# Retention: the high parts of the query and key weight slabs written by a rounding DMA from GpSimd instead of a ScalarE cast

## The reference

```
def _retention(xn, w_in, subln, w_out):
    B, T, _ = xn.shape
    H, Dk, Dv, C = RT_HEADS, RT_KEY_DIM, RT_VAL_DIM, RT_CHUNK
    proj = xn @ w_in
    q, k, v, g = jnp.split(proj, [H * Dk, 2 * H * Dk, 2 * H * Dk + H * Dv], axis=-1)
    ...
        att = jnp.einsum('bhqd,bhkd->bhqk', qq, kk) * decay_intra
        o = (jnp.einsum('bhqk,bhkv->bhqv', att, vv)
             + jnp.einsum('bhqd,bhdv->bhqv', qq, R) * xi[:, :, None])
    ...
    o = _rms(o, subln).reshape(B, T, H * Dv)
    return (jax.nn.silu(g.astype(jnp.float32)) * o).astype(xn.dtype) @ w_out
```

## Time and profile before

| what | value |
|---|---|
| time, median of 3 runs | 1614.63 us (1613.79 to 1614.81) |
| span of the profiled execution | 1611.9 us |
| TensorE busy | 1603.9 us, 100% |
| VectorE busy | 1050.6 us, 65% |
| ScalarE busy | 854.2 us, 53% |
| GpSimd busy | 45.3 us, 3% |

### The profile page before, as it was taken

The page is one execution under the profiler, slowest core; times in us unless marked ns, Lnnn a source line. Parts: engine busy times, 40 slices in busy tenths (PEclk is TensorE's granted clock), DMA queues, the critical chain, the costliest instruction groups (busy, mean ns, idle before and its releaser), DMA issues.

```text
span 1611.9 us, 22737 instructions
## 1 busy us (share of the span) xinstructions
PE 1603.9 (100%) x8789; PEld 1361.9 (84%) x8789; DVE 1050.6 (65%) x1214; ACT 854.2 (53%) x1079; POOL 45.3 (3%) x50
## 2 busy tenths in 40 slices
PE   9999999999999999999999999999999999999999
PEld 7878888978888888888888888888888888888887
DVE  6766656877656776667777666666667554566665
ACT  6654444785444554446775444554445454554443
POOL 2000000000000030000000000000000000000000
PEclk9999999999999999999999999999999999999999
DMA  9635455424555465454345554455545444445540
GB/s 356 226 118 215 178 207 186 164 104 177 191 207 186 153 222 206 184 184 182 121 181 191 201 193 176 177 209 190 194 177 208 160 179 168 172 153 193 203 182 27
DMA packets 42856, 294.29 MB, mean 183 GB/s; under 512 B 4784, under 2 KB 5344, under 8 KB 8736
## 3 DMA queue, kind: packets, MB, share of 16 engines
q1 hardware_dynamic: 39312, 281.04, 47.3%
q0 software_dynamic: 3184, 12.02, 2.3%
q10 hardware_dynamic: 288, 0.20, 0.0%
HBM read 289.18 MB, written 3.15 MB: 181 GB/s over the span
## 4 chain that ended last, share of the span: by engine, by line
PE 98%; DVE 1%; ACT 1%; issue 0%; POOL 0%; DVEq 0%; ACTq 0%; POOLq 0%
PE ups L293 26%; PE accs L260 15%; PE accs L261 15%; PE accs L262 15%; PE ups L296 13%; PE accs L293 2%; PE ups L498 1%; PE accs L296 1%; PE ups L1420 1%; PE accs L449 1%; PE accs L446 1%; PE accs L451 1%; PE ups L2393 1%; DVE wlo L245 1%; PE ups L1046 1%; PE ups L1057 1%
## 5 line engine op out<-in xcount | busy, mean ns | idle before, releaser
L245 DVE TENSOR_TENSOR wlo<-raw,whi 128x2048 fp32r<-128x2048 f32 x263 | 601.5, 2291 | 205.0 <-ACT whi L241 204.9
L293 PE MATMUL ups<-xhl,whi 128*128 128x512 f32 x1824 | 573.2, 396 | 0.0
L241 ACT CAST whi<-raw 128x2048 fp32r<-128x2048 f32 x265 | 505.5, 1910 | 105.7 <-PE accs L262 105.1
L296 PEld LDWEIGHTS ups<-xhl,wlo 128*128 128x128 f32 x1824 | 342.9, 188 | 79.7
L296 PE MATMUL ups<-xhl,wlo 128*128 128x256 f32 x1824 | 358.4, 278 | 0.0
L293 PEld LDWEIGHTS ups<-xhl,whi 128*128 128x128 f32 x1824 | 282.4, 189 | 5.0
L260 PE MATMUL accs<-whi,hidh 128*128 128x512 f32 x692 | 272.4, 394 | 0.0
L261 PE MATMUL accs<-wlo,hidh 128*128 128x512 f32 x692 | 269.9, 390 | 0.0
L262 PE MATMUL accs<-whi,hidl 128*128 128x512 f32 x692 | 269.6, 390 | 0.0
L262 PEld LDWEIGHTS accs<-whi,hidl 128*128 128x128 f32 x692 | 130.0, 188 | 27.6
L260 PEld LDWEIGHTS accs<-whi,hidh 128*128 128x128 f32 x692 | 129.9, 188 | 24.8 <-issue 1.3
(11 more groups left out here) (275 smaller groups left out, 1406.1 us busy)
## 6 DMA issues: line engine op xcount, KB each, us to landing
raw<-weights SPq DMA_DIRECT2D x265, 1024.0 KB, 4.8
gain<-gains POOLq DMA_DIRECT2D x9, 512.0 KB, 4.0
rel_scratch<-sub_rstd POOLq DMA_DIRECT2D x1, 2048.0 KB, 10.9
big<-rel_scratch POOLq DMA_DIRECT2D x1, 1536.0 KB, 10.4
h<-x_in SPq DMA_DIRECT2D x2, 512.0 KB, 5.1
raw<-weights SPq DMA_DIRECT2D x2, 512.0 KB, 6.3
tabs<-consts POOLq DMA_DIRECT2D x1, 1024.0 KB, 6.6
big<-big POOLq DMA_DIRECT2D x2, 384.0 KB, 4.8
```

Source lines behind the costliest of these rows:

```text
L241: nc.scalar.copy(whi[:, m % SPLIT, :], raw[:, m % RAW, :]).then_inc(hi_ready, 1)
L245: nc.vector.tensor_tensor(wlo[:, m % SPLIT, :], raw[:, m % RAW, :], whi[:, m % SPLIT, :].bitcast(F32), ALU.subtract).then_inc(lo_ready, 1)
L293: mm = nc.tensor.matmul(bank, W(whi, n, k, j * P, (j + 1) * P), xhl[:, k, :, :].rearrange("p a n -> p (a n)"), start=k == 0, stop=False)
L296: mm = nc.tensor.matmul(bank[:, 0:T], W(wlo, n, k, j * P, (j + 1) * P), xh[:, k, :], start=False, stop=k == KC - 1)
```

## The change

For the 8 query and key slabs (`ROUNDED`) ScalarE's cast is left out. GpSimd issues a second load of the same slab from HBM, whose destination is `whi`; the DMA converts float32 to float32r on its way. It waits on `slab_used` for the same value that the cast waited for. ScalarE, in the place where the cast stood, waits until that load has landed, and then counts `hi_ready` up by hand. The plain load into `raw` stays, since VectorE needs it for the low part.

```
+        def load_high(pool, m, turn):
+            pool.wait_ge(slab_used, m - SPLIT + 1)
+            pool.dma_start(whi[:, m % SPLIT, :], weights[m]).then_inc(S(f"high_loaded{turn % 2}"), 16)
+
+        def take_high_load(act, m, turn):
+            act.wait_ge(S(f"high_loaded{turn % 2}"), 16 * (turn // 2 + 1))
+            act.wait_ge(raw_loaded[m % RAW], 16 * (m // RAW + 1))
+            act.wait_ge(hi_ready, m)
+            act.sem_inc(hi_ready, 1)
...
+        ROUNDED = [m for m in range(RT_HEADS * RT_SLABS) if m % RT_SLABS in (2, 3)]
...
             for m in range(RT_HEADS * RT_SLABS):
                 u, j = m // RT_SLABS, m % RT_SLABS
-                split_high(act, n_r + m + 2)
+                if m + 2 in ROUNDED:
+                    take_high_load(act, n_r + m + 2, ROUNDED.index(m + 2))
+                else:
+                    split_high(act, n_r + m + 2)
                 if j == 0 and u >= 1:
                     gates(u - 1)
                 if j == 1 and u >= 1:
                     stats(u - 1)
...
+            for turn, m in enumerate(ROUNDED):
+                load_high(pool, n_r + m, turn)
```

## The result

The changed kernel takes 1622.78 us (median of 4 runs, 1620.24 to 1624.42) beside 1614.72 us: ratio 1.0049, 95% interval 1.0033 to 1.0065, so 8 us slower. In a second series on another occasion it took 1623.94 us (5 runs), ratio 1.0055 [1.0041 to 1.0068]. The forecast was 1621.0 within 1616.8 to 1631.

What follows compares the result with a forecast made beforehand. TensorE, busy without a gap, was taken to bound the kernel; its waits in four heads add 6.4 us to the span, 1611.9 to 1618.3, and 2.7 us up to the median gives 1621.0 us, range 1616.8 to 1631.

Steps and rivals of the forecast that it cites:

- The bound: Retention projections: TensorE busy for all 149 us, so removing eight casts, 15.3 us of ScalarE, is worth nothing by itself.
- The shortest distance: Behind the k wait: gated product to `turn_pair`, 1.4 us in head 1, 1.5 in head 2; value copy to slab 21, 2.9.
- The formulas: TensorE's waits: X - 3.1 in head 1, X - 3.2 in head 2, X - 4.6 in head 3.
- X: GpSimd load's time from issue to landing: 5.2 us plus 0.5 for conversion and partial collisions, 5.7; 6.6 in head 0.
- Where X came from: Bounds from plain loads, 5.2 to 7.8 us; k loads were taken to meet no SP load, so near 5.2.
- Head 0: q load behind the last gain load, low part wanted at 1239.24: a wait of X - 6.4, 0.2 us.
- The clock: None of TensorE's waits was thought long enough for the granted clock to fall.
- The 6.4 us: Sum of TensorE's waits: 2.6 (head 1), 2.5 (head 2), 1.1 (head 3) and 0.2 (head 0).
- the 2.7 us between span and median: The 2.7 us by which the median lies above the profiled span, added to 1618.3 to give 1621.0.
- (1): GpSimd's load lands as fast as SP's, X below 4.7, so the time stays the same; chance 0.14.
- (2): Conversion slows GpSimd's load, X from 7 on; at 7.8 the waits are 13.9 us, 1628.5 us; chance 0.22.
- (3): Distances misread, so the wait is absorbed, or relief of ScalarE speeds matmuls; chance 0.06, of which 0.02 faster.

Runs made afterwards that it cites:

- e1: The changed kernel with only the four q slabs loaded by GpSimd, the k slabs cast by ScalarE: 1615.18 us, ratio 1.0003 to the kernel before.
- e9: e7 with head 0's k slab cast by ScalarE, so seven slabs keep GpSimd's load: 1614.6 us, ratio 0.9999 to the kernel before.
- e3: The changed kernel with statistics (ScalarE) and gated product (VectorE) moved ahead of the k wait and subtraction: 1615.47 us, ratio 1.0004 to the kernel before.
- e5: e4 with ScalarE waiting, after its k cast in heads 1 to 3, for the plain load to land: 1630.76 us, ratio 1.01 to the kernel before.
- e8: e3 without its VectorE edit, so only ScalarE's statistics move ahead of the wait: 1618.35 us, ratio 1.0025 to the kernel before.
- e2: The changed kernel with only the four k slabs loaded by GpSimd, q cast by ScalarE: 1630.64 us, ratio 1.0094 to the kernel before.
- e4: The kernel before, casts kept, plus eight plain GpSimd loads of the q and k slabs into an unread region: 1614.63 us, ratio 0.9997.
- e7: e3 with the last gain load moved behind the first q load on GpSimd: 1620.22 us, ratio 1.0035 to the kernel before.

## Why the prediction was right, point by point

**The bound.** TensorE busy without a pause and ScalarE with time to spare: right. In e1 and e9 ScalarE is busy for 7.8 and 12.3 us less between 1228 and 1377, and nothing is gained.

**The shortest distance.** The wait acts through the work behind it, first the statistics and then the gated product, and lands at `turn_pair`. This is shown by e3 (order changed, loads kept), e5 (wait alone) and e8 (each queue holds back its own part). The formulas, with the X of the first profile: 5.0 - 3.1 = 1.9, 5.5 - 3.2 = 2.3 and 5.0 - 4.6 = 0.4 against 2.1, 2.4 and 0.6. They are 0.1 to 0.2 us short at each place, which would fit a handover on the way that I did not count; no run shows which. In e2 they are 3.8, 5.0 and 2.7 against 3.9, 5.1 and 2.9.

**X.** 5.0 to 5.5 us for the k loads of heads 1 to 3, where 5.7 was taken: the allowance for conversion was not needed. This made the forecast 0.7, 0.2 and 0.7 us too high in the three heads, or 0.5, 0.1 and 0.5 with the handover that it left out. (Where the forecast says of the earlier trace rows that the "first second" shows no traffic, it is the first microsecond.)

**Where X came from.** "The k loads fall where no SP load is in transit" is a misreading, and here the forecast had luck. In the kernel before SP's slab of 1269.88 is under way when the k slot of head 1 is released at 1270.92, and the windows from 1272 to 1274 show 426 GB/s. In the changed kernel the k load was alone only because the q load holds back VectorE's subtraction, and SP with it: its slab is issued at 1276.96 there, 3.2 us behind the k load. The forecast had counted that lateness as costing nothing and gaining nothing. In e2, with the q load gone, the same reading fails: X is 6.9 to 8.2.

**Head 0.** The q load took 7.3 us, where 6.6 was taken, behind the gain load and with SP's beside it. By X - 6.4 that is 0.9; the matmuls waited 0.8 and the weight loads 1.2. Its k load took 8.0, and the weight loads waited 0.3 at slab 3. The forecast had 0.2 for the head.

**The clock.** "None is long enough for me to expect the clock to fall" was the wrong sentence. In one of two profiled executions of the changed kernel it fell, behind both longer gaps, and that execution's span is 2.6 us longer; by the mean granted clock (0.998 or less) it probably did in at least six of nine.

**The number.** The 6.4 us are near the measured 8 to 9 in part because errors cancel. X was too long, by 1.6 us over the three heads. Too short were the handovers (0.5 us), head 0 (0.6 by the matmuls, 1.0 to 1.3 by the weight loads) and the clock, which had nothing and takes some 2.6 us where it falls behind both gaps. And the 2.7 us between span and median are not all "what lies around" the span: executions with a span of 1611.9 took 1613.9, so 2.0 lie around it and 0.7 come from a profiled execution that was quicker than the median one. In the changed kernel 1.8 lie around it (1620.3 and 1622.07).

**The rivals.** (1) Not slower needed X below 4.7: it was never below 5.0, though SP's loads took 4.8. The Trainium skill's fit ("DMA: Bandwidth & Descriptors", Anatomy of one DMA) of 4.4 us for 1 MiB from GpSimd is below every one of these loads; these traces decide for 5.0. (2) Slow conversion: not so, by e4. Wherever X was 6.4 us or more, SP's queue moved 0.57 MB or more during the load. That alone does not stretch it, though: in e4 the k load of head 1 landed in 5.0 us with 0.92 MB of SP's in the same stretch, most of it ahead of GpSimd's data. (3) The distances were those read, to 0.2 us, and nothing became faster.

Three things are left open. Why GpSimd's load got only half as much as SP's in e7 is not shown by these runs. Nor is what decides whether the clock falls after a pause of 2 us. And a k load issued earlier, into a buffer of its own, was not tried.

## What to carry to other kernels

Work that is taken off an engine with time to spare is worth nothing, but a longer wait put into its queue is paid by everything behind it: before a cast is replaced by a load, look for what comes next in that queue and how close to its deadline it is. Here the work behind the wait had 1.4 us to spare, while the slab itself had some 7: its low part is ready at 1275.15, and TensorE starts on slab 9 at about 1282.1. If the wait must be there, move what does not depend on it ahead of it, on every engine along the way (e3 against e8). And a transfer's time is not its own: finishing something else sooner can put another load beside it (e2, e7), so check the DMA queues in the window of the one load that someone waits for.

## What the runs showed that I had not expected

- After all seven pauses of TensorE of 2.6 to 5.4 us (three in e2, three in e5, one in e7) the granted clock fell to 0.50 (1.2 GHz), for some 3.4 to 6.8 us; in some of them it fell before the pause had ended. After the four of 2.05 to 2.4 us it fell twice (both in one execution) and stayed at 1.00 twice (both in the other); after those of 0.8 us and less in these two executions, and after the two of 1.1 and 1.2 us in e8, it did not fall. Two pauses of 2 us can therefore cost 4.5 us or some 7 (the gaps, and a span 2.6 us longer).
- A 1024 KB load from GpSimd that converts float32 to float32r landed in 5.0 us, just as a plain one did (5.0), and SP's plain one in 4.8.
- With two loads of SP in flight beside it, the same load took 12.2 us (e7) while SP's queue moved 2.08 MB and GpSimd's 1.08.
